# Moving half-width matmuls into the attention's last steps, and reordering VectorE's queue, in a two-block float32 transformer kernel

## The reference

```python
# second mixer of the first model (swa_sink_mixer)
q, k, v = split(h @ w_in + b_in)              # 16 query heads of 64, 2 key and value heads
s = q @ k.T * 64 ** -0.5, masked to the band of 128
p = exp(s - mx) / (sum(exp(s - mx)) + exp(sink - mx))
return (p @ v).reshape(T, 1024) @ w_out + b_out    # the closing product

# second model (second_block)
z = rms_norm(x) @ w_in        # glu_in, q, k, v, gate_logits
a = causal_depthwise_conv(a_val * sigmoid(a_gate), conv_w, conv_b)     # 31 taps, 1024 channels
q, k = rms_norm(q), rms_norm(k)               # per head of 64
o = attention over the dilations 1, 4 and 16, merged, 16 heads
y_b = o @ w_attn_out;   y_a = silu(rms_norm(a)) @ w_conv_out
x = x + (g_a * y_a + g_b * y_b) @ w_out
x = x + the convolved, gated feed-forward part
```

## Time and profile before

| | |
|---|---|
| median of 3 runs | 2032.04 us (2028.53 to 2035.93) |
| the profiled execution | 2031.16 us, its span 2029.4 us |
| granted TensorE clock, mean | 0.997 of full speed |
| busy: TensorE, VectorE, ScalarE, GpSimd | 1990.0, 1187.2, 855.3, 27.5 us |
| DMA | 188.5 MB, 93 GB/s in the mean |

### The profile page before, as it was taken

The page is one execution under the profiler, slowest core; times in us unless marked ns, Lnnn a source line. Parts: engine busy times, 40 slices in busy tenths (PEclk is TensorE's granted clock), DMA queues, the critical chain, the costliest instruction groups (busy, mean ns, idle before and its releaser), DMA issues.

```text
span 2029.4 us, 25044 instructions
## 1 busy us (share of the span) xinstructions
PE 1990.0 (98%) x9784; PEld 1640.8 (81%) x9784; DVE 1187.2 (59%) x1776; ACT 855.3 (42%) x1374; POOL 27.5 (1%) x34
## 2 busy tenths in 40 slices
PE   7999999999999999999999999999999999999999
PEld 6788898888888778888888987766787888888887
DVE  4344654444456746444445685777797646774664
ACT  4533544233236735423233425677634334442431
POOL 0001100000000000000000000000000000000000
PEclk9999999999999999999999999999999999999999
DMA  5131132324224112333322332222232323332321
GB/s 192 55 123 42 63 103 95 96 81 135 94 83 156 45 50 86 102 95 93 125 94 93 95 103 84 84 83 73 74 94 83 115 83 94 103 95 83 110 98 63
DMA packets 51857, 188.53 MB, mean 93 GB/s; under 512 B 5755, under 2 KB 6011, under 8 KB 51100
## 3 DMA queue, kind: packets, MB, share of 16 engines
q1 hardware_dynamic: 51740, 186.92, 28.4%
HBM read 184.80 MB, written 2.10 MB: 92 GB/s over the span
## 4 chain that ended last, share of the span: by engine, by line
PE 90%; DVE 4%; ACT 3%; issue 2%; DMA 0%; SPq 0%; DVEq 0%; ACTq 0%
PE ps L386 18%; PE ps L388 17%; PE ps L387 17%; PE ps L414 10%; PE ps L416 10%; PE ps L415 10%; DVE WL L1552 1%; PE ps L436 1%; PE ps L801 1%; PE ps L773 1%; PE ps L787 1%; PE ps L568 1%; PE ps L559 1%; PE ps L696 1%; PE ps L751 1%
## 5 line engine op out<-in xcount | busy, mean ns | idle before, releaser
L386 PE MATMUL ps<-HH,WH 128*128 128x512 f32 (+1 forms) x1784 | 667.1, 374 | 4.7 <-DVE HL L1579 1.7
L388 PE MATMUL ps<-HH,WL 128*128 128x512 f32 (+1 forms) x1784 | 655.2, 367 | 0.0
L387 PE MATMUL ps<-HL,WH 128*128 128x512 f32 (+1 forms) x1784 | 654.9, 367 | 0.0
L942 ACT ACTIVATE WH<-WR 128x1024 fp32r<-128x1024 f32 x305 | 321.1, 1059 | 622.2 <-PE ps L388 347.0
L1552 DVE TENSOR_TENSOR WL<-WR,WH 128x1024 fp32r<-128x1024 f32 x305 | 371.9, 1225 | 219.8 <-ACT WH L942 213.2
L386 PEld LDWEIGHTS ps<-HH,WH 128*128 128x128 f32 x1784 | 337.5, 189 | 74.6 <-issue 18.7
L388 PEld LDWEIGHTS ps<-HH,WL 128*128 128x128 f32 x1784 | 337.5, 189 | 55.8
L387 PEld LDWEIGHTS ps<-HL,WH 128*128 128x128 f32 x1784 | 337.8, 189 | 54.2 <-issue 1.9
L414 PE MATMUL ps<-WH,HIDH 128*128 128x512 f32 x624 | 243.2, 390 | 0.0
L416 PE MATMUL ps<-WL,HIDH 128*128 128x512 f32 x624 | 242.8, 389 | 0.0
L415 PE MATMUL ps<-WH,HIDL 128*128 128x512 f32 x624 | 242.8, 389 | 0.0
(11 more groups left out here) (227 smaller groups left out, 2077.4 us busy)
## 6 DMA issues: line engine op xcount, KB each, us to landing
WR<-in_up SPq DMA_DIRECT2D x108, 512.0 KB, 3.6
WR<-in_down SPq DMA_DIRECT2D x86, 512.0 KB, 3.5
WR<-in_in SPq DMA_DIRECT2D x56, 512.0 KB, 3.6
WR<-in_swa_in SPq DMA_DIRECT2D x10, 512.0 KB, 3.9
WR<-in_gla_in SPq DMA_DIRECT2D x9, 512.0 KB, 6.7
WR<-in_gla_v SPq DMA_DIRECT2D x8, 512.0 KB, 3.4
WR<-in_gla_g SPq DMA_DIRECT2D x8, 512.0 KB, 4.8
GAIN<-in_gain SPq DMA_DIRECT2D x4, 1024.0 KB, 7.1
```

Source lines behind the costliest of these rows:

```text
L386: e.matmul(ps, wh, hi[:, c, cols], start=c == 0, stop=False)
L387: e.matmul(ps, wh, lo[:, c, cols], start=False, stop=False)
L388: y = e.matmul(ps, wl, hi[:, c, cols], start=False, stop=c == x.n - 1)
L942: e.activation(x.wh[:, 0:n], m.WR[:, u % RAW, 0:n], AF.Copy).then_inc(*k.mark("whi", u))
```

## The change

`tokens` gets an argument `halves`, with which a call does only one of the two halves. In t_swa's steps p = 6 and 7, four such calls (`ahead`) are put around the transposes. Each does one half of token tile 0 for two of the first four output units: half 0 in step 6, half 1 in step 7. In t_ends_early the first four units of tile 0 are dropped, and the order of the other parts against `between` is new: output 6, two units of tile 1, transposes 14, two units of tile 1, transposes 15, two units of tile 2, output 7, two units of tile 2. ScalarE's order in step 7 becomes: high part, transposes of head 12, exponentials of head 14, transposes of head 13, exponentials of head 15; in step 6 the copy of head 11 moves behind the exponentials of head 13.

In v_second, the cut of the third weight of each step moves behind the weighing of the second head and the values' copy, with the number of taps as before (1 before the weighing, 2 behind the cut). After gate product 15, six items of the list are not taken ahead of the low parts HL; they fall to `more(1000)`.

```diff
-def tokens(e, k, u, n, hi, lo, c0, t, b, ev, need=None, begin=True, end=True):
+def tokens(e, k, u, n, hi, lo, c0, t, b, ev, need=None, begin=True, end=True, halves=(0, 1)):
...
-            for f in range(2):
+            for f in halves:
                 if k.free[b + f]:
                     e.wait_ge(*k.on(*k.free[b + f]))
...
-        for f in range(2):
+        for f in halves:
             w = slice(f * 512, f * 512 + 512)
...
-    part(0, 0, 2, 0)
     between(0)
-    part(0, 2, 2, 0)
+    part(1, 0, 2, 4)
     between(1)
-    part(1, 0, 2, 4)
+    part(1, 2, 2, 4)
     between(2)
-    part(1, 2, 2, 4)
-    part(2, 0, 4, 2)
+    part(2, 0, 2, 2)
+    between(3)
+    part(2, 2, 2, 2)
     part(0, 4, 4, 0)
...
+    def ahead(c, f):
+        w = k.at["swa_out"]
+        tokens(e, k, w + c, 2, m.WOH, m.WOL, c, 0, 0, None, lambda c: [("wol", c)], c == 0, False, (f,))
+
     for p in range(8):
         score(p)
         if p >= 2:
             out(p - 2)
         if p < 6:
             product(e, k, u + 4 + p, m.HH, m.HL, 2, 0, ev="ae", c1=4)
+            if p >= 1:
+                turn(2 * p - 2)
+            product(e, k, u + 4 + p, m.HH, m.HL, 2, 0, ev="ae", c0=4)
+            if p >= 1:
+                turn(2 * p - 1)
+        else:
+            if p == 6:
+                ahead(0, 0)
             turn(2 * p - 2)
+            ahead(2 if p == 6 else 0, p - 6)
             turn(2 * p - 1)
+            if p == 7:
+                ahead(2, 1)
...
         if n == 0:
             out(6)
-            turn(14)
-        if n == 1:
-            turn(15)
-        if n == 2:
+        elif n < 3:
+            turn(13 + n)
+        else:
             out(7)
...
-        expo(2 * p)
+        if p < 7:
+            expo(2 * p)
         if p >= 2:
             high(p - 2)
         if p >= 1:
             turn(2 * p - 2, 0)
             turn(2 * p - 2, 1)
-        if p >= 6:
+        if p == 7:
+            expo(2 * p)
             turn(2 * p - 1, 0)
         expo(2 * p + 1)
         if p < 6:
             evac(p + 4)
-        if 1 <= p < 6:
+        if 1 <= p < 7:
             turn(2 * p - 1, 0)
...
         more(3)
         weigh(i)
-        v_cut(e, k, u + 5)
-        more(3)
+        more(1)
         weigh(i + 1)
         if c < 8:
             evac_v(c)
+        v_cut(e, k, u + 5)
+        more(2)
+        if c < 8:
             norm_qk(c)
...
     for j in range(5, 16):
         v_cut(e, k, u + j + 3)
-        more(6)
+        if j < 15:
+            more(6)
```

More of the change, by code:

```diff
@@ L723, in t_swa @@
             product(e, k, u + 4 + p, m.HH, m.HL, 2, 0, ev="ae", c1=4)
-        if p >= 1:
+            if p >= 1:
[6 more added lines that the diff above has]
+                ahead(0, 0)
             turn(2 * p - 2)
-        if p < 6:
-            product(e, k, u + 4 + p, m.HH, m.HL, 2, 0, ev="ae", c0=4)
-        if p >= 1:
+            ahead(2 if p == 6 else 0, p - 6)
             turn(2 * p - 1)
+            if p == 7:
+                ahead(2, 1)
     def between(n):
```

## The result

The changed kernel takes 2019.36 us (median of 5 runs, 2017.92 to 2022.2) against 2032.04 us before: ratio 0.9944, 95% interval 0.9929 to 0.9959. The forecast was 2018.5, the range 2014.5 to 2024.5. The profiled execution has a span of 2017.3 us, 12.1 less than before.

The account below looks back on a forecast made before the run. TensorE, busy 98% of the span, was taken as the bound, so only its pauses, work or clock could pay. Gains of 7.6 + 3.8 + 0.4 + 1.7 = 13.5 us took 2032.0 to 2018.5 us, range 2014.5 to 2024.5.

Parts of the forecast that it names:

- The sum: Whole kernel: gains of 7.6 + 3.8 + 0.4 + 1.7 = 13.5 us, giving 2018.5 us.
- Part A: End of the second mixer's attention: early halves and ScalarE's new order gain 7.6 us.
- The layout: Step-by-step timing of TensorE's new order at the mixer's end, from 703.65, giving the 7.6 us gain.
- wait for the fourth weight: Mixer's step 6: TensorE newly waits 1.8 us for the fourth output weight's low part, replacing the 2.50 pause.
- wait behind head 15: Closing product: the third tile's first twelve matmuls newly wait 0.6 us for ScalarE's copy out of bank 3.
- the cross-check of 6.9: Mixer's end: comparing old and new idle time and low-clock loss gives 6.9 us, kept as the near bound.
- Part B: Last block's attention: values' copy before the weight gains 3.8 us in the first step, 0.4 in the sixth.
- part C: Product after the last block's attention: six taps moved behind the low parts remove the 1.70 us wait.
- The clock rival: Clock falls anyway at the mixer's end or last block's first attention step: 2019.7 to 2022.6 us; chance 0.2.
- New waits: Rival at the mixer's end: the 1.8 us wait grows through head 11's chain, total 2023 us; chance 0.09.
- other queues: Rival: gain given back to VectorE's taps or the weight transfers, 2027 to 2034 us; chance 0.05.
- slower: Rival: low clock from the pause at 706.5 lasts through the closing product, 0.3% slower from 39 us on; chance 0.03.

Follow-up runs that it names:

- scalar_only: bc_only with ScalarE's new order in steps 6 and 7, TensorE's old order and no early halves: 2021.03 us, ratio 0.9953.
- c_only: Kernel before with only the six taps left behind the low parts HL in v_second: single run 2028.4 us.
- b_only: Kernel before with only the third weight's cut moved behind the values' copy in v_second: single run 2030.47 us.
- filler: Kernel before with 12 matmuls that nobody reads added between the transposes of heads 12 and 13: 2029.12 us, ratio 0.9992.
- a_only: Changed kernel with both v_second edits taken back, leaving the early halves and new TensorE and ScalarE orders: 2028.46 us, ratio 0.9986.
- bc_only: Kernel before with both v_second edits put in, without halves or new orders at the mixer's end: 2027.28 us, ratio 0.9981.

## Why the prediction was right

- **The sum.** 13.5 us forecast, 12.7 measured in the medians (10.1 the second time), 12.7 by the places (6.65 + 3.66 + 0.7 + 1.7). That the first medians meet the sum by places is in part luck: the places come from a profile of before with low clock in both pauses, worth 2.56 and 1.13 us, and not every run of before has it. The forecast took both as certain (2.9 and 1.2). Without them the places would give about 9.0, an estimate; the fastest runs give 10.5.
- **Part A**, 7.6 forecast, 6.65 measured. The layout held step by step when 0.83 is taken off the times after: wait for the fourth weight 1.65 (1.8 forecast), head 13's transposes at 715.7 (715.2), output step of pair 6 through at 720.0 (719.4), wait behind head 15 0.40 (0.6), last output step at 730.6 (729.8), extra weights at 735.3 (734.4). The term that was mis-sized is the hand-over between unlike matmuls, some 0.1 each, which the layout rounded away (the first six matmuls took 1.50 for 1.4, the last twelve 3.00 for 2.8); the cross-check of 6.9 was nearer.
- **Whose gain it is** was read wrongly in one respect. The prediction priced the halves and ScalarE's order as one part under the name of the halves. The layout used both, but ScalarE's order alone takes the long pause from 4.39 to 0.45 us, while the halves alone leave one of 2.52. Laying out TensorE's old order beside ScalarE's new one would have shown it beforehand: the expectation of scalar_only did so and came to 32 to 33 us, 33.45 measured. A reader of the forecast would have credited the halves with 7.6 us; on top of ScalarE's order they gave 0.14.
- **Part B**, 3.8 forecast for the first step, 3.66 measured, the clock included (2.53 where the clock does not fall, by c_only; 2.65 was the forecast's figure for a clock that falls in spite of B, which did not happen in any profile with B); **part C** 1.70 as forecast, the taps' later end stayed covered (no wait at the fifth unit).
- **The clock rival.** It did not occur in the places named: none of the seven profiles with the halves shows a low clock at the mixer's end. But one argument against it falls: the 2.50 us pause brought no fall in the profile of before, yet in b_only, c_only and filler it did. And a pause's length alone does not decide it: the 0.96 us one in the first block stands just before low clock in eight of 14 profiles. The rule cited from the Trainium skill, page "TensorE: Matmul & The Clock Gate", section "A second HAM failure mode: psum-queue depth-cycling", is not borne out in the mixer's end by the short pauses left there (1.65, 0.40); that it has no part in the first block is not shown.
- **New waits, other queues, slower:** the waits were where they were put; nothing gave the gain back.

What stays open: whether a_only's and bc_only's many runs with a low mean clock, most likely from the first block as in their profiles (a_only: 8 of 12 runs at a mean clock of 0.997 or below; bc_only: 6 of 12 at 0.996 or below) are chance. The changed kernel had 3 of 11 at 0.997 or below. No run separates that.

## What to carry to other kernels

When an engine waits for a neighbour's copy, lay out the neighbour's queue first: an order of ScalarE that empties PSUM before it starts the next exponentials gave 6.44 of 6.58 us by itself, and matmuls moved into the pause added something to it only after their own input (a weight's low part made earlier on VectorE) came in time. When two edits aim at one wait, try each without the other: the same halves are worth 3.85 us alone and 0.14 behind the other edit. Where single steps of 1 to 7 us are at stake in 2030, compare the same stretch in two profiles, with its idle time and its clock, since the median of the changed kernel moved by 2.8 us between two sets of 5 and 6 runs (2019.36, 2022.17). And price a low clock as part of the pause that can bring it, but with a chance: of four profiles with the 2.7 us pause, one had none.

## What the runs showed of the hardware that was not expected

The granted clock fell in two places of the first block without a long pause. In a_only TensorE is busy all the way, first with full matmuls, then for 3.2 us with matmuls of 33 rows (the row at 55.70), and in these the clock goes to 0.50, for 6.8 us. The same code at this place showed a low clock in 6 of 13 profiles and not in the others, among them that of the changed kernel. That the 33-row matmuls bring it is not shown. The other place is near 213 us: there TensorE is idle for 0.96 or 0.97 us in all 14 profiles, between rows of small matmuls (in the changed kernel's profile the one at 210.71 is behind it), and a low stretch of 3.4 or 6.8 us begins 0.1 to 2.3 us behind the pause in eight of them. The longer pauses of 1.65 and 1.70 us had none behind them in any profile.

The cost is seen in the spread: with the same code (before, 23 runs on one chip) the runs lie between 2028.5 (mean clock 0.999) and 2035.9 us (0.995). The low clock of the mixer's end and of the last block is a part of that spread.
